# Hybrid transformer block on one core: the value product of the last stage with the values stationary instead of the coefficients

## What is computed

```python
def one_chunk(args):
    xc, ic, gc = args
    u_g = peer_u[ic]
    h = jax.nn.gelu(jnp.einsum('chkd,cd->chk', u_g, xc).astype(f32), approximate=False) * gc
    v_g = peer_v[ic]
    return jnp.einsum('chk,chkd->cd', h.astype(peer_v.dtype), v_g)
...
h = h + peer_ffn(xn, peer_wq[l], peer_subkeys[l], peer_u[l], peer_v[l])
return rmsnorm(h, normf_g)
```

## Time and profile before

| what | us |
|---|---|
| device time, median of 3 runs | 1049.22 (1048.21 to 1049.79) |
| span of the profiled execution | 1046.5 |
| median less that span (what lies around the span) | 2.7 |
| TensorE busy with matmuls | 1037.5 (99%) |
| VectorE, ScalarE, GpSimd busy | 708.5, 639.7, 475.8 |
| value stage, first matmul to start of the last two units | 692.3 to 1035.1 |
| last two units, last norm and stores | 1035.1 to 1046.5 |

### The profile page before, as it was taken

The page is one execution under the profiler, slowest core; times in us unless marked ns, Lnnn a source line. Parts: engine busy times, 40 slices in busy tenths (PEclk is TensorE's granted clock), DMA queues, the critical chain, the costliest instruction groups (busy, mean ns, idle before and its releaser), DMA issues.

```text
span 1046.5 us, 21868 instructions
## 1 busy us (share of the span) xinstructions
PE 1037.5 (99%) x6864; PEld 908.6 (87%) x6864; DVE 708.5 (68%) x1634; ACT 639.7 (61%) x1259; POOL 475.8 (45%) x228
## 2 busy tenths in 40 slices
PE   9999999999999999999999999999999999999997
PEld 8998899998898888888888888888888888888886
DVE  7765645446669999696888888865555555555554
ACT  7773575555565555657888888865454454454544
POOL 4685543883369888887777777730000000000000
PEclk9999999999999999999999999999999999999999
DMA  7463312555545555454444444455555555555553
GB/s 262 160 214 111 122 44 83 184 183 217 190 135 192 187 183 195 170 185 170 160 160 155 152 156 159 160 182 187 194 197 188 197 192 189 200 188 194 195 188 139
DMA packets 52134, 180.98 MB, mean 173 GB/s; under 512 B 5811, under 2 KB 7859, under 8 KB 51964
## 3 DMA queue, kind: packets, MB, share of 16 engines
q1 hardware_dynamic: 51660, 179.87, 50.4%
q10 hardware_dynamic: 432, 0.55, 0.2%
HBM read 179.34 MB, written 1.06 MB: 172 GB/s over the span
## 4 chain that ended last, share of the span: by engine, by line
PE 86%; DVE 12%; ACT 1%; DMA 0%; issue 0%; ACTq 0%; POOL 0%; DVEq 0%
PE PS L439 17%; PE PS L910 11%; PE PS L911 11%; PE PS L912 11%; PE PS L443 8%; PE PS L429 4%; PE PS L430 4%; PE PS L431 4%; PE PS L807 3%; PE PS L865 2%; PE PS L815 1%; DVE PS L1463 1%; DVE arena L1824 1%; PE PS L866 1%; DVE arena L1816 1%; DVE arena L1812 1%
## 5 line engine op out<-in xcount | busy, mean ns | idle before, releaser
L1358 POOL TENSOR_TENSOR lo<-raw,hi 128x1024 fp32r<-128x1024 f32 x191 | 463.0, 2430 | 190.2 <-ACT hi L957 178.3
L957 ACT CAST hi<-raw 128x1024 fp32r<-128x1024 f32 x331 | 346.7, 1048 | 189.3 <-DMA raw<-in_v_units 170.5
L439 PE MATMUL PS<-xb,hi 128*128 128x512 f32 x1088 | 279.3, 398 | 1.0 <-ACT arena L1243 1.0
L1417 DVE TENSOR_TENSOR lo<-raw,hi 128x1024 fp32r<-128x1024 f32 x140 | 171.7, 1226 | 148.7 <-ACT hi L957 148.7
L439 PEld LDWEIGHTS PS<-xb,hi 128*128 128x128 f32 x1088 | 194.9, 189 | 38.1 <-issue 2.4
L910 PE MATMUL PS<-hi,xb 128*128 128x512 f32 x512 | 199.4, 389 | 0.0
L912 PE MATMUL PS<-lo,xb 128*128 128x512 f32 x512 | 199.2, 389 | 0.0
L911 PE MATMUL PS<-hi,xb 128*128 128x512 f32 x512 | 199.2, 389 | 0.0
L443 PEld LDWEIGHTS PS<-xb,lo 128*128 128x128 f32 x1088 | 148.4, 190 | 11.0
L443 PE MATMUL PS<-xb,lo 128*128 128x256 f32 x1088 | 151.4, 282 | 0.0
L910 PEld LDWEIGHTS PS<-hi,xb 128*128 128x128 f32 x512 | 96.1, 188 | 20.5 <-issue 0.4
(11 more groups left out here) (315 smaller groups left out, 1375.1 us busy)
## 6 DMA issues: line engine op xcount, KB each, us to landing
raw<-in_u_units SPq DMA_DIRECT2D x128, 512.0 KB, 3.2
raw<-in_v_units SPq DMA_DIRECT2D x128, 512.0 KB, 3.2
raw<-in_w_in_units SPq DMA_DIRECT2D x43, 512.0 KB, 3.3
raw<-in_w_q_units SPq DMA_DIRECT2D x16, 512.0 KB, 3.2
raw<-in_w_proj_units SPq DMA_DIRECT2D x8, 512.0 KB, 3.2
raw<-in_w_out_units SPq DMA_DIRECT2D x8, 512.0 KB, 3.2
arena<-bias_rows SPq DMA_DIRECT2D x2, 512.0 KB, 4.8
arena<-in_subkeys_t SPq DMA_DIRECT2D x1, 1024.0 KB, 5.4
```

The lines of the kernel that those rows point to most:

```text
L439: mm(PS[:, bank, :], hi[:, s, P * k:P * k + P], both[:, k].rearrange("p s t -> p (s t)"), start=(k == 0), stop=False, skip_group_check=True)
L957: nc.scalar.copy(hi[:, j, :], raw[:, j, :]).then_inc(hi_made, 1)
L1358: nc.gpsimd.tensor_tensor(lo[:, w, :], raw[:, w, :], hi[:, w, :].bitcast(F32), ALU.subtract).then_inc(lo_pool, 1)
L1417: V.tensor_tensor(lo[:, w, :], raw[:, w, :], hi[:, w, :].bitcast(F32), ALU.subtract).then_inc(lo_dve, 1)
```

## The change

The value product swaps its operands. `hi` or `lo` of a value unit is stationary, 128 channels at a time, and the coefficients of all 256 tokens move: `gh` and `gl` side by side (512 columns), then `gh` alone with `lo` (256 columns). The result is now turned (channels by tokens) and takes all eight PSUM banks, one for each chunk `c` of 128 channels, with the sum of the `gl` product in a bank's upper half. The residual no longer goes through TensorE at the start. At the end VectorE adds for each chunk the upper half and then the lower half to `xT`, TensorE turns the chunk with two transposes into four banks, and the last norm runs on those. It is reordered: the squares of the first columns of both token tiles, then of the second columns, then ScalarE scales the first columns of each tile and VectorE the second.

```diff
+            def wide_value(j, c, start=False):
+                return mm(PS[:, V_BANKS[c], 0:2 * T],
+                          hi[:, (U_V + j) % 4, P * c:P * c + P], xb[:, j].rearrange("p s t -> p (s t)"), start=start, stop=False,
+                          skip_group_check=True)
+
+            def low_value(j, c, last=False):
+                return mm(PS[:, V_BANKS[c], 0:T], lo[:, (U_V + j) % 4, P * c:P * c + P], xb[:, j, 0, 0:T],
+                          start=False, stop=last, skip_group_check=True)
...
             def whole_unit(i, j):
-                operands_ready(i, j)
-                for b in range(4):
-                    last = accumulate(j, b)
-                last.then_inc(unit_done, 1)
+                value_ready(i, j)
+                for c in range(KT):
+                    wide_value(j, c)
+                value_lows(j, lo_dve, 4 * i + (U_V + j + 1 + LO_DVE_V))
...
-            for b in range(4):
+
+            def turned_out(c):
+
+                pe.wait_ge(tail_made, max(c, 1 if c < 4 else 3) + 1)
+                for n in range(NT):
+                    last = nc.tensor.transpose(PS[:, OUT_AT[c // 4][n], P * (c % 4):P * (c % 4) + P],
+                                               xT[:, c, P * n:P * n + P], ident)
+                last.then_inc(fin_ps, 1)
+
+            for c in range(KT):
                 for j in (2, 3):
-                    if b == 0:
-                        operands_ready(final, j)
-                    last = accumulate(j, b, j == 3)
-                last.then_inc(acc_done, 1)
+                    if c == 0:
+                        value_ready(final, j)
+                    wide_value(j, c)
+                if c == 0:
+                    pe.wait_ge(lo_dve, 4 * final + (U_V + 3 + 1 + LO_DVE_V))
+                low_value(2, c)
+                low_value(3, c, last=True).then_inc(acc_done, 1)
+                if c >= 3:
+                    turned_out(c - 3)
+            for c in range(KT - 3, KT):
+                turned_out(c)
...
+            def first_columns(n):
                 act.wait_ge(fin_inv, n + 1)
-                nc.scalar.activation(rms[:, 3 * n:3 * n + 1], rms[:, 3 * n:3 * n + 1], ACT.Sqrt).then_inc(fin_root, 1)
...
+                root = rms[:, 2 + n:3 + n]
+                nc.scalar.activation(root, root, ACT.Sqrt).then_inc(fin_root, 1)
+                act.wait_ge(fin_root, n + 1)
+                act.wait_ge(gained, n + 1)
+                nc.scalar.activation(result[:, n, 0:512], PS[:, OUT_AT[0][n], :], ACT.Copy, scale=root).then_inc(fin_act, 1)
+
+            for h in range(2):
+                for n in range(NT):
+                    squares(h, n)
+            for n in range(NT):
+                first_columns(n)
+                act.wait_ge(fin_act, n + 1)
+                nc.scalar.dma_start(out_tiles[n, :, 0:512], result[:, n, 0:512]).then_inc(stored, 16)
...
+            for c in range(KT):
+                dve.wait_ge(acc_done, c + 1)
+                both = PS[:, V_BANKS[c], :]
+                V.tensor_tensor(xT[:, c, :], both[:, T:2 * T], xT[:, c, :], ALU.add).then_inc(tail_half, 1)
+                dve.wait_ge(tail_half, c + 1)
+                V.tensor_tensor(xT[:, c, 0:T], both[:, 0:T], xT[:, c, 0:T], ALU.add).then_inc(tail_made, 1)
```

More of the change, by code:

```diff
@@ L402, in _ @@
                     load(v_t[4 * i + j], (U_V + j) % 4)
-            for n, (tile, h) in enumerate(((0, 0), (0, 512), (1, 512))):
-                sp.wait_ge(fin_sb, n + 1)
-                sp.dma_start(out_tiles[tile, :, h:h + 512], result[:, tile, h:h + 512]).then_inc(stored, 16)
+            for tile in range(NT):
+                sp.wait_ge(fin_sb, tile + 1)
+                sp.dma_start(out_tiles[tile, :, 512:D], result[:, tile, 512:D]).then_inc(stored, 16)
             sp.wait_ge(stored, 64)
@@ L898, in _ @@
                     gated_unit(i, j)
[L899 to L912, removed]
@@ L928, in _, with value_lows @@
[L928 to L932, removed]
-                for b in range(4):
-                    last = accumulate(j, b)
-                last.then_inc(unit_done, 1)
+            def value_lows(j, lo_sem, lo_count):
+                pe.wait_ge(lo_sem, lo_count)
+                for c in range(KT):
+                    last = low_value(j, c)
+                last.then_inc(unit_done, 1)
@@ new lines, in whole_unit @@
+            def whole_unit(i, j):
+                value_ready(i, j)
+                for c in range(KT):
+                    wide_value(j, c)
+                value_lows(j, lo_dve, 4 * i + (U_V + j + 1 + LO_DVE_V))
+            value_ready(0, 0)
+            for c in range(KT):
+                if c == V_BANKS.index(U_BANKS[0]):
+                    pe.wait_ge(coef_made, HALF + 1)
+                if c == V_BANKS.index(U_BANKS[3]):
+                    pe.wait_ge(coef_made, HALF + 2)
+                wide_value(0, c, start=True)
@@ L936, in _ @@
+            value_lows(0, lo_pool, LO_POOL_V + 1)
+            value_ready(0, 1)
+            for c in range(KT):
+                wide_value(1, c)
+            value_lows(1, lo_pool, LO_POOL_V + 2)
             whole_unit(0, 2)
@@ L1987, in _ @@
[L1987 to L1994, removed]
-            V.tensor_tensor(PS[:, 2, :], PS[:, 2, :], gain_all[:, 0:512], ALU.mult).then_inc(gained, 1)
@@ new lines, in _, with mean_inverse @@
+            link(V.tensor_scalar(rms[:, 0:2], rms[:, 0:2], D * RMS_EPS, None, ALU.add))
+            def mean_inverse(n):
+                total = rms[:, 2 + n:3 + n]
+                dve.wait_ge(fin_sq, 3 + n)
+                link(V.tensor_scalar(total, total, rms[:, n:n + 1], 1.0 / D, ALU.add, ALU.mult))
+                V.reciprocal(total, total).then_inc(fin_inv, 1)
+            for n in range(NT):
+                mean_inverse(n)
+            for n in range(NT):
+                dve.wait_ge(fin_root, n + 1)
+                V.scalar_tensor_tensor(out=result[:, n, 512:D], in0=PS[:, OUT_AT[1][n], :], scalar=rms[:, 2 + n:3 + n],
+                                       in1=gain_all[:, 512:D], op0=ALU.mult, op1=ALU.mult).then_inc(fin_sb, 1)
```

45 lines of the change are left out of this document (15 added, 30 removed).

## The result

| what | before | changed |
|---|---|---|
| device time, median | 1049.24 us (4 runs, 1048.21 to 1049.79) | 1061.83 us (4 runs, 1061.12 to 1062.79) |
| ratio, 95% interval | | 1.0122 [1.0108, 1.0137] |
| span of the profiled execution | 1046.5 us | 1061.0 us |

The changed kernel is 1.2% slower, 12.6 us by the medians. The forecast was 1061.8 us. The total came out in part by luck: the sum left out a lost clock, worth some 0.7 us in the median, and put 0.9 us too much around the span, and the two nearly cancel. So the profile matters more here than the total.

The account below looks back on a forecast made before the run. TensorE was taken to bound the kernel, busy 99% of the span. Span 1046.5 - 0.1 (start) + 9.2 (units) + 3.5 (end) = 1059.1 us, plus 2.7 around it, gave 1061.8 us; range 1057.5 to 1066.

Parts of the forecast that it names:

- The unit: Value stage: a unit goes from 2.720 to 2.793 us, the U stage's figure; +9.2 us over 126 units.
- the narrow matmuls pay most: Value unit: 256-column matmuls cost 0.119 us each where their columns at 2.4 GHz are 0.107.
- The start of the stage: Value stage start: without 16 transposes TensorE idles some 1.8 us waiting for `gl` and starts sooner; -0.1 us.
- The clock at the start: Idle stretch ahead of the value stage: granted clock assumed to hold, so nothing charged.
- The end: Last two units to span end: additions, turning and serial scaling no longer covered; 14.85 against 11.36 us, +3.5 us.
- The first two stores delaying the last two: Kernel's end: named with a lower clock in the gaps as what could make the end's cost 5 us.
- Nothing got a harder deadline: Value stage: loads, ScalarE and VectorE feeding TensorE get no harder deadline; cost zero.
- What lies around the span: Outside the profiled span: median of before lies 2.7 us above it, added to the predicted span of 1059.1 us.
- the unit of 2.85: Rival, value stage: units at the U stage's second-half price, +16.8 us, 1069.4 us in all; chance 0.09.
- Cost by columns: Rival, value stage: 256 columns cost 0.113 us, unit stays 2.720, only the end changes; 1052.6 us; chance 0.06, shared with the formula.
- The third: Rival, value stage: narrow matmuls at 0.110 us, unit 2.694, 3.3 us given back; 1049.3 us, not slower; chance 0.03.
- The Trainium skill's formula: Rival, value stage: units 2.590 us before and 2.600 now, +1.3 us over 126; 1053.9 us; chance 0.06, shared with cost by columns.

Follow-up runs that it names:

- the first experiments: The first group of four follow-up experiments on one chip; the kernel before, timed beside them, took 1049.15 us (15 runs).
- 128-column run: Changed kernel with the eight narrow matmuls of every value unit cut from 256 to 128 columns, all 16 stationary loads kept; 1056.28 us (one run).

## Why the prediction came out, step by step

- **The unit: right.** 2.793 us were taken from the U stage and 2.793 were measured; 126 units gave 9.12 us for the forecast 9.2. The words beside it were partly wrong: "the narrow matmuls pay most". They pay the same 0.0134 as all others; sixteen equal ones cost 2.775. What is special is the wide pass behind them, 1.84 us in place of 8 x 0.2267 = 1.81.
- **The start of the stage: not told apart from noise.** The forecast had it 0.1 us sooner; in the profile it is 0.25 later (692.51 against 692.26), and in the variants of the changed kernel it goes from 692.16 to 692.38, and to 693.03 in one.
- **The clock at the start: wrong.** "I do not charge a lower clock for the idle stretch" rested on the earlier trace rows, where the clock held for over 2 us behind the last matmul. In the profiled execution an idle stretch of 1.87 us was followed by up to 1.63 us of lost time, and filling it with matmuls went with a median 0.7 us lower. The row showed one case. The ends of the profiles show how much it varies: the same clock falls 1.6 us behind the last TensorE work of the changed kernel (end 1054.21) and 3.5 us behind that of the kernel before (1040.84). First the changed kernel, then the kernel before:

```profile
1055.00:1056.00 1.00, 0.00 (x0) 0.00 (x0) 0.80 (x5) 0.97 (x4) 0.00 (x0) 0.92 0.00 0
```

```profile
1044.00:1045.00 1.00, 0.00 (x0) 0.00 (x0) 0.00 (x0) 0.00 (x0) 0.00 (x0) 0.70 0.85 328
```

The clock is lost in some executions only. My estimate, from three of nine profiles and two of four spans, is that the term should have been a chance of about a third to a half of +1.6 us.

- **The end: right in size (3.5 and 3.53), but with one of two limits.** The steps came within 0.15 us of the forecast: the last squares started 8.14 us behind the start of the last two units (forecast 8.01), the second root 10.73 (10.73), the last scalings 10.97 (10.96). The forecast let the serial second root and scaling set the end, and removing that chain alone brought nothing, because the first store and then 1 MB at the transfers' rate set the same end. "The first two stores delaying the last two" stood only among the bounds. That the two limits agree here to less than 0.1 us, so that the 3.15 us of the kernel before still gave the right end, is luck.
- **Nothing got a harder deadline: nearly right.** No supplier was late inside the stage. The last `lo` costs up to 1 us in one execution (with the transposes in the gap) and 0.03 in the profile of the changed kernel, so at the last two units the margin is thin.
- **What lies around the span: wrong, and it hid the clock.** 2.7 us was the median less one profiled span. In the runs with both figures it is 1.8 (1062.79 and 1061.0), but for six executions of the kernel before without its transposes, with 2.6 to 2.9. The profiled span of before was most likely a short one: among 15 executions beside the first experiments the spans go from 1046.5 to 1047.8. The 0.9 us too much stood in for the clock's share of the median, and that is luck.

Of the rivals, the unit of 2.85 falls with the measured 2.793. (By the figures printed with it, 126 units at 2.85 would add 16.4 us and not 16.8.) The 128-column run points to why the U stage's wide pass costs 1.90 there: 128-column matmuls go before it, and 1.90 appeared in the value stage with them. Cost by columns falls: 256 columns cost 0.120, not 0.113. The third, narrow matmuls at the transposes' pitch, falls as well, although the 0.11 us of the 128-column run is that pitch.

The Trainium skill's formula (TensorE: Matmul & The Clock Gate, "Back-to-back issue gap") of N / 2.4 GHz plus about 2.5 ns, which the section gives for single matmuls apart from a stream with stationary loads, would have made the units 1.3 us dearer. The trace has 9.1. It does fit the float16 matmuls of the gates, which start 0.056 us apart (690.04, 690.10 and 690.15 in the timeline without the residual), but none of the float32 matmuls of the value stage.

## What to carry to other kernels

With the same columns, fewer and wider matmuls win: swapping operands so that 12 matmuls of 512 become 8 of 512 and 8 of 256 cost 0.073 us a unit, and a stage of the same shape in the same trace told that to the nanosecond. Work that TensorE does in a wait may be worth having even when it costs and gains no path time: with the wait left empty the clock fell in three of nine profiles, with it filled in none of three, which is a hint and no proof. At a kernel's end, look at when the first store starts and how many bytes follow; a shorter chain of scalings behind it may gain nothing.

## What the hardware showed that was not expected

- Float32 matmuls cost their columns at 2.4 GHz plus 0.0134 us at 256, 384 and 512 columns alike (0.120, 0.173, 0.2267), with one stationary load of 128 columns each. At 128 columns it is 0.11 us and not 0.067.
- A wide matmul behind narrow ones is slower for several matmuls: a pass of eight takes 1.84 us behind 256-column ones, 1.90 behind 128-column ones, against 8 x 0.2267 = 1.81. Behind an idle stretch of 0.82 us the same steps showed, with the first at 0.337 us. That a stationary load loses its lead there would fit all of it, but no row shows the cause.
- Around an idle stretch of 1.87 us TensorE's granted clock fell in three of nine profiles (0.79 in the mean over the next 8 us, and 0.50, its lower level, for part of them). In the changed kernel it fell when TensorE had been busy again for 1.5 us, in the other two sooner (0.80 and 0.82 in the mean from 690 to 694). It held in all three profiles in which transposes or matmuls filled the stretch, and six of nine would make that no rare thing by chance.
- Four stores of 256 KB at the end moved at some 385 GB/s and ended 4.5 to 4.6 us after the first was issued; two alone ended after 3.1 us.
- It stays open why the kernel before has executions with spans of 1046.2 to 1046.5 us and others of 1046.9 to 1047.8, and why the last `lo` came 1 us late in one profile.
